# Out-weights of the second expert loaded into dead buffers, one projection piece instead of two for the keys, gathers regrouped, and VectorE copying what was loaded ahead

## What is computed

```python
q = x @ w_in[:, :512]             # 8 heads of 64, heads 0..3 share key/value head 0, heads 4..7 head 1
k, v = x @ w_in[:, 512:640], x @ w_in[:, 640:768]
...
hb = xb @ w_exp_in[e] + b_exp_in[e]                 # [tokens of e, 2048]
g = min(hb[:, :1024], 7); u = clip(hb[:, 1024:], -7, 7)
a = g * sigmoid(1.702 * g) * (u + 1)
y = a @ w_exp_out[e] + b_exp_out[e]                 # [tokens of e, 1024]
out[token] += gate[token, e] * y
```

## Time and profile before

| | |
|---|---|
| median of 3 runs | 1464.12 us (1462.02 to 1468.61) |
| profiled execution | 1462.36 us |
| its span, first to last instruction | 1460.5 us |
| PE matmul busy | 1306.9 us (89%) |
| PE weight load busy | 810.3 us (55%) |
| VectorE busy | 466.8 us (32%) |
| ScalarE busy | 504.1 us (35%) |
| GpSimd busy | 221.5 us (15%), all before 510 us |
| DMA moved | 494.40 MB, mean 339 GB/s |

### The profile page before, as it was taken

How to read it: one execution, slowest core, us unless ns; L and a number is a source line. 1 busy time by engine, 2 the same in 40 slices (tenths; PEclk the granted TensorE clock), 3 DMA queues, 4 the chain that set the end, 5 groups by cost and what they waited for, 6 DMA issues and landing times.

```text
span 1460.5 us, 25988 instructions
## 1 busy us (share of the span) xinstructions
PE 1306.9 (89%) x9475; PEld 810.3 (55%) x9476; DVE 466.8 (32%) x916; ACT 504.1 (35%) x790; POOL 221.5 (15%) x129
## 2 busy tenths in 40 slices
PE   7999999999999997787889898989888988898886
PEld 7787999878999853333333433344343434343433
DVE  2755777664534961111101110111011111111112
ACT  5566666555657422112111311131121212131222
POOL 6772122007774300000000000000000000000000
PEclk9999999999999999999999989999999999999999
DMA  9432667755463778999999999999999999999996
GB/s 342 171 101 64 185 186 234 281 194 182 165 231 116 270 331 373 431 432 430 431 431 404 431 431 431 415 432 431 431 431 431 420 431 431 431 418 431 431 431 268
DMA packets 105321, 494.40 MB, mean 339 GB/s; under 512 B 6609, under 2 KB 56129, under 8 KB 80481
## 3 DMA queue, kind: packets, MB, share of 16 engines
q1 hardware_dynamic: 103795, 491.50, 82.8%
q10 hardware_dynamic: 1486, 2.34, 0.4%
HBM read 492.76 MB, written 1.06 MB: 338 GB/s over the span
## 4 chain that ended last, share of the span: by engine, by line
PE 61%; DMA 25%; DVE 5%; ACT 4%; issue 3%; POOL 1%; SPq 0%; DVEq 0%; ACTq 0%; POOLq 0%
DMA big_mem<-in_w_exp_in 25%; PE ps L1071 18%; PE ps L1115 8%; PE ps L595 6%; PE ps L597 5%; PE ps L596 5%; PE ps L1054 3%; PE ps L1129 1%; PE ps L813 1%; PE ps L814 1%; PE ps L815 1%; PE ps L1138 1%; PE ps L1102 1%; ACT x L1740 1%; PE ps L615 1%
## 5 line engine op out<-in xcount | busy, mean ns | idle before, releaser
L1071 PE MATMUL ps<-big_mem,ring_mem 128*32 128x512 f32 (+1 forms) x2304 | 375.7, 623 | 46.5 <-DMA big_mem<-in_w_exp_in 46.4
L1071 PEld LDWEIGHTS ps<-big_mem,ring_mem 128*32 128x32 f32 (+1 forms) x2304 | 115.1, 124 | 288.6 <-issue 212.5
L1115 PE MATMUL ps<-big_mem,x 128*32 128x256 f32 (+1 forms) x1888 | 183.4, 436 | 4.7 <-ACT x L1740 3.7
L595 PE MATMUL ps<-hT_hi,w_hi 128*128 128x256 f32 x600 | 171.3, 285 | 1.3 <-DVE hT_lo L1836 1.3
L1724 ACT ACTIVATE ring_mem<-ring_mem 128x256 f32<-128x256 f32 (+1 forms) x36 | 17.7, 493 | 441.6 <-DVE ring_mem L2344 441.6
L596 PE MATMUL ps<-hT_lo,w_hi 128*128 128x256 f32 x600 | 169.7, 283 | 0.0
L597 PE MATMUL ps<-hT_hi,w_lo 128*128 128x256 f32 x600 | 169.7, 283 | 0.0
L1054 PEld LDWEIGHTS ps<-ring_mem,h 128*128 128x128 f32 x1024 | 124.0, 191 | 57.8 <-issue 57.8
L2344 DVE TENSOR_SCALAR ring_mem<-ps 128x256 f32<-128x256 f32 (+1 forms) x36 | 18.7, 520 | 406.6 <-PE ps L1071 406.6
L1795 ACT ACTIVATE big_mem<-ahead 128x2048 f32<-128x2048 f32 x62 | 115.0, 1902 | 85.2 <-DMA ahead<-in_w_exp_in 82.6
L1054 PE MATMUL ps<-ring_mem,h 128*128 128x96 f32 x1024 | 141.6, 281 | 0.0
(11 more groups left out here) (431 smaller groups left out, 1748.9 us busy)
## 6 DMA issues: line engine op xcount, KB each, us to landing
big_mem<-in_w_exp_in SPq DMA_DIRECT2D x97, 2048.0 KB, 23.1
big_mem<-in_w_exp_out SPq DMA_DIRECT2D x64, 2048.0 KB, 19.0
ahead<-in_w_exp_in SPq DMA_DIRECT2D x31, 2048.0 KB, 21.7
ring_mem<-in_w_in SPq DMA_DIRECT2D x14, 2048.0 KB, 7.7
ring_mem<-in_w_up SPq DMA_DIRECT2D x44, 512.0 KB, 4.9
ring_mem<-in_w_down SPq DMA_DIRECT2D x5, 2048.0 KB, 10.7
ring_mem<-in_w_out SPq DMA_DIRECT2D x4, 2048.0 KB, 7.7
ring_mem<-in_w_branch_a SPq DMA_DIRECT2D x1, 2048.0 KB, 7.3
```

The lines of the kernel that those rows point to most:

```text
L595: mm(out, hi, x_hi, start=start, stop=False)
L1071: last = mm(out, stationary, weights[:, f, w * q:w * (q + 1)] if m > XS else weights[:, :, w * q:w * (q + 1)], start=start, stop=stop)
L1115: last = mm(ps[m * q:m * (q + 1), 4 + at // XS, 0:w], aT[:, k % n, k // n, :], wout[:, k, w * q:w * (q + 1)], start=(k == 0), stop=(k == K ...
```

## The change

It makes six edits.

1. The host puts the query heads in the order 0, 4, 1, 5, 2, 6, 3, 7 (the rows of `w_out` and the sinks alike). A pair then uses both key heads, one on each half of the rows, so that one piece holds both keys, nothing is broadcast, and 31 pieces become 30.
2. The first six k of `wout` for expert 1 are loaded behind `wout` of expert 0 into three places that are no longer used (`second_homes`: the upper half of slot 1, `late`, two rows of `bc`); VectorE copies them over at the end of expert 0, and k 6 and 7 are loaded straight into place.
3. `ahead` of expert 2 is issued before what is left of expert 1's `wout`. From expert 2 on the sequence of transfers is the old one.
4. VectorE instead of ScalarE copies `ahead` to `win[6:8]`, between the `own` row and the copy of y (in passes of a many-pass expert, in the last).
5. PE gathers three blocks behind the first product, one behind `way_back`, one behind `turn_a`, one behind `second`, and two behind `combine`; `load_next` stands at the end.
6. ScalarE's copy of the first five gathered blocks comes behind `a_in`.

```diff
+        second_homes = [v.rearrange("p (k n) -> p k n", n=D) for v in (slot[1][:, 2 * D:4 * D], late[:], bc[:, 0:2, :].rearrange("p a d -> p (a d)"))]
-        PIECES1, STEPS1 = 31, 27
+        PIECES1, STEPS1 = 30, 26
...
             if p < 6:
-                return cols8[1][:, :, HEAD * (p - 4):HEAD * (p - 3)].unsqueeze(2).broadcast_to([P, KD, 2, HEAD])
-            if p == 6:
-                return cols8[1][:, :, P:2 * P]
+                return cols8[1][:, :, P * (p - 4):P * (p - 3)]
...
+            for k in range(2):
+                sp.dma_start(second_homes[k], wout_x[1, :, 2 * k:2 * k + 2, :]).then_inc(s["second_in"], 16)
+            sp.wait_ge(s["h1_ready"], T)
+            sp.dma_start(second_homes[2], wout_x[1, :, 4:6, :]).then_inc(s["second_in"], 16)
...
+            def load_ahead(e, cur):
+
+                sp.wait_ge(win_in[-1], 16 * e)
+                sp.sem_inc(s["refill_due"], 1)
+                sp.dma_start(ahead[:], one(win_x, cur, *WIN_PARTS[-1])).then_inc(s["ahead_in"], 16)
...
+            load_ahead(2, sp.value_load(order[0:1, 2:3], min_val=0, max_val=E - 1))
+            sp.wait_ge(s["y_part"], KD * others + KD)
+            sp.sem_inc(s["refill_due"], 1)
+            sp.wait_ge(s["second_in"], 16 * 3)
+            sp.dma_start(wout[:, 6:8, :], wout_x[1, :, 6:8, :]).then_inc(s["second_in"], 16)
+            with sp.Fori(2, E - 1) as e:
+                before = nth(e - 1)
+                cur = nth(e)
+                load_wout(load_win(bass.ds(before, 1), cur), cur)
+                load_ahead(e + 1, nth(e + 1))
...
-            first_T(6, ps[:, 3, 0:SEQ])
...
-                gather(0, EARLY)
-                load_next()
+                gather(0, 3)
                 for b, (at, m) in enumerate(blocks):
...
                     way_back(b, at)
+                gather(3, EARLY - 1)
                 for b, (at, m) in enumerate(blocks):
...
                     turn_a(at, m)
+                gather(EARLY - 1, EARLY)
+                pe.wait_ge(s["aT_ready"], base + len(blocks))
+                second(blocks, landed_all)
                 pe.wait_ge(s["xT_ready"], 2 * turn + 3)
                 gather(EARLY, EARLY + 1)
-                pe.wait_ge(s["aT_ready"], base + len(blocks))
-                second(blocks, landed_all)
-                gather(EARLY + 1, EARLY + 2)
                 for b, (at, m) in enumerate(blocks):
                     pe.wait_ge(s["y_ready"], base + b + 1)
                     combine(b, at, m, base + b)
-                gather(EARLY + 2, KD)
+                gather(EARLY + 1, KD)
+                load_next()
...
-                with act.If(e < E - 1):
-                    act.wait_ge(s["ahead_in"], 16 * e + 16)
-                    for z, k in enumerate(range(*WIN_PARTS[-1])):
-                        last = run(win[:, k, :], ahead[:, z, :], ACT.Copy)
-                    last.then_inc(win_in[-1], 16)
...
                 following(own_row)
+                closing()
                 for b, (at, m) in enumerate(blocks):
...
+                def take_ahead():
+
+                    with dve.If(e < E - 1):
+                        dve.wait_ge(s["ahead_in"], 16 * e + 16)
+                        for z, k in enumerate(range(*WIN_PARTS[-1])):
+                            last = v.tensor_copy(win[:, k, :], ahead[:, z, :])
+                        last.then_inc(win_in[-1], 16)
+                    dve.nop()
...
+                with dve.If(e < 1):
+                    dve.wait_ge(s["second_in"], 16 * 3)
+                    for k in range(2):
+                        last = v.tensor_copy(wout[:, 2 * k:2 * k + 2, :], second_homes[k])
+                    last.then_inc(wout_in[0], 16)
+                    dve.wait_ge(s["second_in"], 16 * 4)
+                    v.tensor_copy(wout[:, 4:6, :], second_homes[2]).then_inc(wout_in[1], 16)
```

More of the change, by code:

```diff
@@ L288, in uses @@
             return len([i for i in range(n % 3, n + 1, 3) if i != UP])
-        used = dict(enumerate([("piece_lo", c) for c in (4, 7, 11, 15, 19, 23, 30, 31)] + [("lo3", NF // 2)]
+        used = dict(enumerate([("piece_lo", c) for c in (4, 6, 10, 14, 18, 22, 29, 30)] + [("lo3", NF // 2)]
                               + [("lo3", NF // 2 + c) for c in range(1, 6)] + [("lo1", NF // 2 + 6)]
@@ L315, in split1 @@
             v = W1_PLACE[p][:, part, :]
-            return v.rearrange("p (k n) -> p k n", k=KD if p < 7 else 2)
-        def split1_out(part, p):
-            if p in (4, 5):
-                return W1_PLACE[p][:, part, :].rearrange("p (k z n) -> p k z n", k=KD, z=2)
-            return split1(part, p)
+            return v.rearrange("p (k n) -> p k n", k=KD if p < 6 else 2)
         first_piece = {w2_hi.name: early_piece[:, 0, :], w2_lo.name: early_piece[:, 1, :]}
@@ L492, in expert, with nth @@
                     sp.dma_start(wout[:, a:b, :], one(wout_x, cur, a, b)).then_inc(wout_in[n], 16)
-            expert(slice(0, 1), 1)
+            def nth(e):
+                return sp.value_load(order[0:1, bass.ds(e, 1)], min_val=0, max_val=E - 1)
+            others = load_win(slice(0, 1), 1)
             sp.wait_ge(s["order_ready"], 1)
-            with sp.Fori(2, E) as e:
-                before = sp.value_load(order[0:1, bass.ds(e - 1, 1)], min_val=0, max_val=E - 1)
-                cur = sp.value_load(order[0:1, bass.ds(e, 1)], min_val=0, max_val=E - 1)
-                sp.wait_ge(win_in[-1], 16 * e)
-                sp.sem_inc(s["refill_due"], 1)
-                sp.dma_start(ahead[:], one(win_x, cur, *WIN_PARTS[-1])).then_inc(s["ahead_in"], 16)
-                expert(bass.ds(before, 1), cur)
+            load_ahead(2, sp.value_load(order[0:1, 2:3], min_val=0, max_val=E - 1))
[8 more added lines that the diff above has]
+                load_ahead(e + 1, nth(e + 1))
+            before = sp.value_load(order[0:1, E - 2:E - 1], min_val=0, max_val=E - 1)
+            cur = sp.value_load(order[0:1, E - 1:E], min_val=0, max_val=E - 1)
+            load_wout(load_win(bass.ds(before, 1), cur), cur)
             for t in range(T):
@@ L517, in low1 @@
                 pool.wait_ge(s["piece_hi"], p + 1)
[L518 removed]
+                half = split1(1, p).shape[1] // 2
                 for k in (slice(0, half), slice(half, 2 * half)):
[L520 removed]
+                    last = nc.gpsimd.tensor_tensor(split1(1, p)[:, k], raw1(p)[:, k], split1(0, p)[:, k].bitcast(F32), ALU.subtract)
                 last.then_inc(s["piece_lo"], 1)
@@ L1407, in _ @@
             projected(3, two(m1["qT"], 2), 1)
-            for p in range(6, 11):
+            for p in range(6, 10):
                 high1(p)
-                if p == 9:
+                if p == 8:
                     nc.scalar.preload_act_table(ACT.Exp)
             exps(0)
+            high1(10)
             high1(11)
             high1(12)
-            high1(13)
             for u, name in enumerate((None, "vr", "gate")):
-                p = 11 + 4 * u
+                p = 10 + 4 * u
                 turned(u)
@@ L1438, in _ @@
             high_cat(3)
-            for p in range(25, 27):
+            for p in range(24, 26):
                 high1(p)
@@ L2424, in after, with at_last, closing @@
                     return choose
+                def at_last(p):
+                    def closing():
+                        with dve.If(more <= p):
+                            take_ahead()
+                        dve.nop()
+                    return closing
                 with dve.If(extra < 1):
-                    one_pass(GROUPS[0], cur, 0, next_expert)
+                    one_pass(GROUPS[0], cur, 0, next_expert, take_ahead)
                 with dve.If(extra > 0):
                     with dve.If(extra < 2):
-                        one_pass(GROUPS[1], cur, 0, next_expert)
+                        one_pass(GROUPS[1], cur, 0, next_expert, take_ahead)
                     with dve.If(extra > 1):
@@ L2464 @@
     given = {n: np.ascontiguousarray(inputs[n]) for n in _INS}
+    w_in, w_out, sinks = (np.array(inputs[n]) for n in ("w_in", "w_out", "attn_sinks"))
+    w_in[0, :, 0:HALF] = w_in[0, :, 0:HALF].reshape(D, 2, 4, HEAD).transpose(0, 2, 1, 3).reshape(D, HALF)
+    w_out[0, 0:HALF] = w_out[0, 0:HALF].reshape(2, 4, HEAD, D).transpose(1, 0, 2, 3).reshape(HALF, D)
+    given |= {"w_in": w_in, "w_out": w_out, "attn_sinks": np.ascontiguousarray(sinks.reshape(2, 4).T.reshape(1, 8))}
     for n in ("w_exp_in_2", "w_exp_out_2"):
```

88 lines of the change are left out of this document (44 added, 44 removed).

## The result

The changed kernel took 1481.38 us (median of 4, 1480.02 to 1481.81), the kernel before in the same set 1465.10 (1462.02 to 1468.61): ratio 1.0112, 95% interval 1.0093 to 1.0130. The forecast was 1473.1, +0.6%; it came out at +1.1%, slower as forecast and inside the wide range of 1455 to 1486, but above the forecast's own range of 1466 to 1478: the loss is 16.3 us where 9.0 were forecast. The profiled execution took 1481.81 us, its span is 1480.0.

What follows compares the result with a forecast made beforehand. Arithmetic was taken to bound until some 525 us, then the weight stream at 431 GB/s. Terms -2.7 - 7.3 + 19.6 - 0.6 = +9.0 on 1462.36 gave 1471.4, in medians 1473.1 us; own range 1466 to 1478, wide 1455 to 1486.

Steps and rivals of the forecast that it cites:

- One key piece less: Before the first scores: six pieces of 24 matmuls instead of seven, all that follows earlier, -2.7 us.
- Out-weights of expert 1 ahead: Stream at 525 to 535 us: three loads fill its idle time, so it runs earlier, -7.3 us.
- the sign that one of the first two steps is wrong: Profile after: the refills of expert 3 are not some 10 us earlier.
- VectorE instead of ScalarE takes `ahead`: End of pass: copies delay y and `combine` by 4.9 us; gather block and `load_next` add 1.1; first product +3.9 us late.
- the 19.6 forecast: Sum over the four three-block experts: +4.9 us each from late first product, gathers and clock, +19.6 us.
- Gathers behind the transposes: Between long product and second product: two gather blocks and ScalarE's token copy leave the chain, -0.7 us per three-block expert.
- The clock: Ahead of each three-block expert: PE idle some 5 us, clock drops earlier, over part of `combine`, gathers, bias products, +1.7 us.
- The tail: Last expert: no `ahead` to wait for, second product could start earlier but its second half waits for weights, -0.6 us.
- cold restarts throughout: Rival, chance 0.20: clock low from `combine` into first weights at four three-block experts, +7 us each, sum +17.4, 1481.5 us.
- The stream wins: Rival, chance 0.14: the 3 MB in the idle stretch are kept, long experts are not late, -10.6, 1453.5 us.
- The preload gives nothing: Rival, chance 0.06: the gap only moves, as PE paces expert 2's refills, +16.3, 1480.4 us.
- The gaps behind the long experts: Profile after: the stream stands still 5 to 7 us behind each of the four long experts, instead of 2.

Runs made afterwards that it cites:

- experiment 1: Changed kernel with VectorE's copy of `ahead` moved behind its copy of y: 1469.60 us, 1.0033 of the kernel before.
- 4: Changed kernel with ScalarE copying `ahead` behind its pass again, VectorE's copy dropped: 1463.37 us, 0.9993 of the kernel before.
- experiment 2: Changed kernel with `load_next` moved from the end of the pass to behind the first three gather blocks: 1457.16 us, 0.9943 of the kernel before.
- experiment 3: Changed kernel with `load_next` behind the first three gather blocks and VectorE's copy of `ahead` behind its copy of y: 1456.29 us, 0.9947 of the kernel before.
- experiment 9: Changed kernel with `load_next` behind the first three gather blocks and ScalarE copying `ahead` as before: 1454.76 us, 0.9935 of the kernel before.
- experiment 7: Kernel before with one edit, `load_next` moved from behind the first five gather blocks to the end of the pass: 1497.76 us, ratio 1.0226.
- experiment 13: Changed kernel with `load_next` behind the first three gather blocks and ten constant-tile products at the end of the pass: 1470.53 us, 1.0064 of the kernel before.
- experiment 6: Changed kernel with `load_next` behind the first three gather blocks, without the out-weights of expert 1 ahead: 1462.19 us, 0.9987 of the kernel before.
- experiment 11: Changed kernel with ten products of a constant tile ahead of `load_next` at the end of every pass: 1528.70 us, 1.0425 of the kernel before.

## Why the prediction came out as it did

The medians give the way from before to the changed kernel in four steps: 1464.3, key piece and preload 1457.9 (-6.4), VectorE's copy ahead of y 1463.2 (+5.3), gathers behind the transposes 1457.2 (-6.0), `load_next` at the end 1481.4 (+24.2). Another order gives other prices: taken out of the changed kernel alone, VectorE's copy ahead of y is worth 11.8 us (experiment 1) or 18.0 (4), the place of the loads 24.2 (2), and both together no more than 25.1 (3) or 26.6 (9).

*One key piece less*, -2.7: measured -3.2. Right.

*Out-weights of expert 1 ahead*, -7.3: measured -5.0; and with the key piece -6.4 where -10.0 stood. The gap in front was filled as said, but I wrote that the in-weight refills behind it are hardly delayed. Expert 2's first refill goes out at 557.98, the stream is at 52 GB/s from 555 to 560, and part of the gain stays there. The first refill of expert 3 goes out 1.3 us earlier than before (586.04 against 587.35) and not 10, which was named as the sign that one of the first two steps is wrong; `ahead` of the first three-block expert lands 7.3 us earlier (737.11).

*VectorE instead of ScalarE takes `ahead`.* The step that failed is its last: `load_next` at 0.73 us, the pause seen ahead of the transposes, and 1.1 for it and a gather block together, "PE's sequencer runs ahead of some of that". That 0.73 was what stuck out from under 2.47 us of queued gather blocks. At the end of the pass the sequencer has just waited for y and for the halves of `combine`, and seems to be hardly ahead of the engine; moving the line lengthened the pause there by 2.67 us (experiment 7), and covering it gave back 24.2 (experiment 2). And I counted it at four experts only: "for a one-block expert that is free". It was free one pass at a time, but a two-block pass has no reserve. Here is the start of one, and that of the expert behind it, in the changed kernel:

```profile
691.14 1.07 PE L1088 MATMUL ps<-ring_mem 128*64 128x512 bf16 x4 [3.31 <-issue]
...
725.33 0.41 PE L1088 MATMUL ps<-ring_mem 128*32 128x512 bf16 x4 [1.60 <-issue]
```

That is 34.2 us against the stream's 29.2, so the next begins late. The first half of the step, y 4.9 us late, is seen as described at three of the four three-block experts (4.50, 5.10, 4.56) and, once the loads are covered, at all four. What the two halves did there, in us at the four experts in order, by the profiled executions:

| | before | experiment 2 | changed |
|---|---|---|---|
| `ahead` landed, to the first product | 4.9, 4.9, 4.9, 4.9 | 8.7, 8.7, 8.7, 8.7 | 10.6, 11.0, 11.0, 11.0 |
| `ahead` landed, to the refill of the out-weights | 42.1, 41.6, 41.1, 40.9 | 43.1, 42.3, 43.4, 42.4 | 45.7, 46.2, 46.0, 46.2 |

In the second row the changed kernel loses 18.4 us at the four, near the 19.6 forecast. But with the loads covered, y as late and the first product 3.8 us late (3.9 were forecast), it is 5.4: most of the late start is won back, since the long product then takes 22.5 to 23.6 us where it took 23.8 to 25.0, and the way to the second product is shorter. The other 13.0 come with the uncovered loads. That the sum at the four is right is luck. Outside them the forecast had -10.0 ahead of the first, nothing between, and -0.6 at the end; measured are -7.3, +4.2 and +4.2. The four parts give the 19.5 us of the spans.

*Gathers behind the transposes*, -0.7 each: at the first three-block expert the way from the end of the long product to the second is 771.61 to 776.57, 4.96 us against 6.06, -1.1. Over the kernel it is -3 to -6 rather than -2.8, since all passes gain.

*The clock*, +1.7 each. At the first three-block expert the long product took 24.02 us against 25.01, and at 740 to 760 us both kernels have the same granted clock, 0.83. At the other three the clock fell at the place named, behind the wait for y; the changed kernel at `combine` ahead of the second, then the kernel before at the same work:

```profile
892.00:897.00 5.00, 4.09 (x24) 2.73 (x24) 0.69 (x2) 0.00 (x0) 0.00 (x0) 0.50 0.99 426
```

```profile
890.00:895.00 5.00, 3.49 (x32) 1.73 (x31) 1.26 (x5) 2.79 (x2) 0.00 (x0) 1.00 1.01 433
```

0.50 is the lower level. `combine` and the gathers took 1.9 us longer there, the pause behind them was 1.4 us shorter than at the first (2.23 to 2.28 against 3.67), and the long product was no slower than before (23.9 to 24.2 against 23.8 to 24.6). In the other passes, each of which begins behind a pause, the granted clock is 0.90 against 0.97 at 600 to 720 us, and this the forecast left out. By experiment 13 about half of the 24.2 us go with the clock.

*The tail*, -0.6: from the last refill of the four to the end of the span 178.5 us against 174.3, +4.2. That stretch holds more than the last expert; the last one too starts behind such a pause (1.60 us, its first product at 1452.62 with no wait for weights), and no run takes it by itself.

*The rivals.* The one of cold restarts throughout gave 1481.5 us, and the time was 1481.4. That is a hit by number alone: it had +28 us at the four three-block experts and none outside, where 18.4 stood at the four. Its condition was seen at three of them, `combine`, gathers and bias products at the low clock, but its price of 7 us each was not. The Trainium skill ("TensorE: Matmul & The Clock Gate", section "HAM oscillation — how this bites in real kernels") says that idle gaps make the next burst start cold. The rows agree in kind: behind 3.67 us of pause the eight bias products took 1.61 us, behind 0.97 us of it (experiment 9) 0.98. But behind a pause of 1.40 us in the kernel before they took 1.62 too (at 1247.11), so the pause alone does not tell. In size, by the estimate of experiment 13, the clock is about half of the 24.2 us and the length of the pauses the other half. "The stream wins" is near what the kernel does once `load_next` is covered: it forecast 1453.5, experiment 2 gave 1457.2, and experiment 9, with the copy back on ScalarE, 1454.8. "The preload gives nothing" forecast 1480.4, and that is near by number alone: experiment 6 shows that the preload gives 5.0. The gaps behind the long experts, 5 to 7 us by the forecast, are the 7.4 above.

Not settled: why 2.40 us of products ahead of the loads hide nothing of them (experiment 11). The Trainium skill ("TensorE: Matmul & The Clock Gate", section "Architectural detail: the array is 16× 32×32, not 1× 128×128") gives TensorE's queue a depth of 64. The ten products are 20 records and as many weight loads, which would not fill it; with `combine` and the last gathers ahead of them it is 44 and 44. No run here tells what held the sequencer. One reading would fit these runs and is not shown: the loads cost little where the sequencer is ahead, as it is behind the long first product, and behind a wait it does not get ahead, whatever short products follow. At the end of a pass 2.64 us of `combine` and gathers lie in front of the loads as it is, more than the 2.47 us at their old place, and hide as little as the ten products.

## What to carry to other kernels

A control instruction is priced by its place. The pause that a profile shows at its old place is what sticks out from under the work there, and says nothing of its length; just behind a semaphore wait far more of it appeared, in nearly every pass. Idle time of an engine that waits for the stream anyway costs little as long as it only takes the place of that waiting (experiment 3), and costs once the waiting is used up (experiment 7), so delays must be added up over consecutive passes before any is called free. Look at each place where a mechanism should act: at the first of the four the wait for y was missing, at the other three it was there. And a number that comes out near by a mechanism that is not in the trace is not a confirmation.

## What the runs showed of the hardware

Three loads of a register on TensorE's sequencer, two needing the first, lengthened the pause ahead of a three-block expert from 1.41 to 4.08 us when they stood at the end of the pass (experiment 7); in the changed kernel the pauses ahead of the next product were mostly 1.6 to 3.7 us. One load left 0.45 us ahead of the first three-block expert; ten products (20 records, 2.40 us) put ahead of the three shortened the pauses in the sum not at all (99.2 us against 88.9). VectorE copied 128x2048 fp32 from SBUF to SBUF in 1.223 us, ScalarE in 1.902. Behind waits of 4.5 to 5.1 us the same 24 matmul records of `combine` and gathers took 4.6 us in place of 2.6.
